# First products started on column quarters of the memory, with filler products ahead of them, and the squares of memory and x in other places

## The reference

```python
mem_n = rmsnorm(mem, mem_norm)                  # 256 memory tokens x 2048
for layer in range(2):
    h = rmsnorm(x, g[0]); mix = even_mixer(...) or odd_mixer(...)
    x = x + rmsnorm(mix, g[1])
    h = rmsnorm(x, g[2])
    k = mem_n @ wk[layer]; v = mem_n @ wv[layer]   # inside memory_cross_attention
    x = x + rmsnorm(memory_cross_attention(h, mem_n, wq, wk, wv, wo), g[3])
    h = rmsnorm(x, g[4]); x = x + rmsnorm(swiglu(h, ...), g[5])
```

## Time and profile before

| | before |
|---|---|
| median of 3 runs | 2846.91 us (2846.89 to 2847.23) |
| the profiled execution | 2846.54 us |
| its span in the trace | 2844.8 us, so 1.7 us lie around it |
| PE busy | 2826.8 us, 99% of the span |
| DVE busy | 2207.7 us, 78% |
| ACT busy | 1586.4 us, 56% |
| weights and other data moved | 593 MB, 208 GB/s mean |

### The profile page before, as it was taken

One profiled execution on the slowest core, in us unless ns is written; L12 is line 12 of the kernel. 1 busy time (PEld: TensorE's weight loads), 2 busy tenths in 40 slices (PEclk: granted clock), 3 DMA queues, 4 the chain that ended last, 5 costly groups with the idle time before them and its releaser, 6 DMA issues. The chain is left out here.

```text
span 2844.8 us, 31833 instructions
## 1 busy us (share of the span) xinstructions
PE 2826.8 (99%) x12990; PEld 2346.7 (82%) x12990; DVE 2207.7 (78%) x1517; ACT 1586.4 (56%) x1432; POOL 53.0 (2%) x109
## 2 busy tenths in 40 slices
PE   9999999999999999999999999999999999999998
PEld 7888888888888888888888888778888888888887
DVE  7888787669699988885456877899599888986444
ACT  7666555546356655664444765556456656655443
POOL 0000000000000000000000000000000000000000
PEclk9999999999999999999999999999999999999999
DMA  7674754656466546547555654656566556456552
GB/s 273 230 279 168 275 198 176 244 181 243 177 221 237 184 173 235 214 170 282 192 193 174 214 192 167 237 188 236 205 214 223 183 215 232 170 190 271 195 194 94
DMA packets 240241, 593.01 MB, mean 208 GB/s; under 512 B 9009, under 2 KB 9041, under 8 KB 223585
## 3 DMA queue, kind: packets, MB, share of 16 engines
q1 hardware_dynamic: 233792, 532.72, 52.5%
q0 software_dynamic: 5424, 47.78, 4.3%
q10 hardware_dynamic: 880, 10.49, 0.9%
HBM read 569.98 MB, written 20.97 MB: 208 GB/s over the span
## 5 line engine op out<-in xcount | busy, mean ns | idle before, releaser
L1183 DVE TENSOR_TENSOR w_lo<-wide,w_hi 128x2048 fp32r<-128x2048 f32 x556 | 1261.8, 2290 | 371.4 <-ACT w_hi L604 367.8
L604 ACT ACTIVATE w_hi<-wide 128x2048 fp32r<-128x2048 f32 x556 | 1060.2, 1915 | 478.6 <-PE ps L1934 367.3
L1934 PE MATMUL ps<-w_hi,act_hi 128*128 128x512 f32 x3272 | 877.3, 391 | 0.3 <-ACT w_hi L617 0.2
L1934 PE MATMUL ps<-w_lo,act_hi 128*128 128x512 f32 x3272 | 872.3, 389 | 0.9 <-DVE w_lo L1183 0.9
L1934 PE MATMUL ps<-w_hi,act_lo 128*128 128x512 f32 x3272 | 871.3, 389 | 0.0
L1934 PEld LDWEIGHTS ps<-w_lo,act_hi 128*128 128x128 f32 x3272 | 613.9, 188 | 130.5 <-DVE w_lo L1183 3.1
L1934 PEld LDWEIGHTS ps<-w_hi,act_lo 128*128 128x128 f32 x3272 | 614.4, 188 | 128.1
L1934 PEld LDWEIGHTS ps<-w_hi,act_hi 128*128 128x128 f32 x3272 | 611.9, 188 | 127.9 <-issue 1.9
L1187 DVE TENSOR_TENSOR wide<-wide,wide 128x2048 f32<-128x2048 f32 x114 | 261.1, 2290 | 5.6 <-DVE w_sum L1187 0.5
L1138 ACT ACTIVATE act_hi<-mid 128x256 fp32r<-128x256 f32 x80 | 33.4, 418 | 243.1 <-PE ps L1934 243.1
L604 ACT ACTIVATE w_hi<-w_sum 128x2048 fp32r<-128x2048 f32 x38 | 73.0, 1922 | 102.3 <-DVE w_sum L1187 90.7
(11 more groups left out here) (266 smaller groups left out, 1655.2 us busy)
## 6 DMA issues: line engine op xcount, KB each, us to landing
wide<-in_ffn_w_gate SPq DMA_DIRECT2D x88, 1024.0 KB, 8.4
wide<-in_ffn_w_up SPq DMA_DIRECT2D x88, 1024.0 KB, 7.3
wide<-in_ffn_w_down SPq DMA_DIRECT2D x88, 1024.0 KB, 4.8
wide<-in_odd_w_in SPq DMA_DIRECT2D x48, 1024.0 KB, 5.6
wide<-in_xattn_wk SPq DMA_DIRECT2D x32, 1024.0 KB, 7.8
wide<-in_xattn_wv SPq DMA_DIRECT2D x32, 1024.0 KB, 6.7
wide<-in_even_w_in SPq DMA_DIRECT2D x32, 1024.0 KB, 6.8
wide<-in_xattn_wq SPq DMA_DIRECT2D x32, 1024.0 KB, 5.5
```

The costliest lines, as they stand in the source:

```text
L604: nc.scalar.activation(w_hi[:, c % W_SLOTS, :], src, ACT.Copy).then_inc(hi_done, 2)
L1183: nc.vector.tensor_tensor(w_lo[:, c % W_SLOTS, :], src, w_hi[:, c % W_SLOTS, :].bitcast(F32), ALU.subtract).then_inc(lo_done, 2)
L1934: return nc.tensor.matmul(dst, lhs, rhs, start=start, stop=stop, skip_group_check=loose)
```

## The change

It has three parts. **Fillers:** PE issues products of a tile of ones into bank 0, of which nothing is kept: 4 ahead of the gain vectors' product, 3 ahead of the first transposes, 6 behind them. **Quarters:** the memory comes in four column quarters of 512 KB with both token halves, each ahead of its chunk; chunk 0 comes in two halves. PE turns tiles 4s to 4s+3 of both token halves (two tiles of 256 tokens to a bank), and in the new `opening_mem` takes each chunk for both token halves at once. ACT and DVE alternate two tiles of memory with half a chunk. **Squares:** ACT squares memory half 0 between chunks 2 and 3, half 1 behind chunk 3 as before; DVE takes the two `var` of the memory behind the first token sums instead of ahead of chunk 4. The squares of x go behind the splits of chunk products 8 and 10 of strip 1.

```diff
 # SP, in load(n, src)
-                if n == 1:
-                    for b in range(1, 4):
-                        memory(b)
-                    sp.wait_ge(mem_in[1], 16)
-                elif n < WIDE and n:
+                if 2 <= n < WIDE:
                     sp.wait_ge(wide_full[n - 2], 16)
-                if n == 3:
-                    sp.dma_start(memx[:, 1, :], mem[P:2 * P, :]).then_inc(mem_in[4], 16)
+                if n < 4:
+                    memory(n)
...
+                if n == 0:
+                    sp.dma_start(dst[:, 0:2, :], src[:, 0:2, :]).then_inc(first_half, 16)
+                    dst, src = dst[:, 2:4, :], src[:, 2:4, :]
 # ACT
-            def round_mem(m, banks=range(4)):
+            def round_mem(b, halves):
                 act.wait_ge(vec_done, 1)
...
+                for j in range(2):
+                    bank = WORK + 2 * (b % 2) + j
+                    act.wait_ge(work_full[bank], plan["mem_norm"]["rf"] + b // 2 + 1)
+                    for k in range(2):
+                        t = 4 * b + 2 * j + k
+                        ins = nc.scalar.activation(act_hi[:, t, :], ps[:, bank, k * T:(k + 1) * T], ACT.Copy,
+                                                   scale=vec[:, 16 + t:17 + t])
                     ins.then_inc(hi_ev, 1)
+                    split_halves(halves, b, (j,))
...
-            round_mem(1)
+            for s in range(4):
+                round_mem(s, first)
+                if s == 2:
+                    for landed_mem in mem_in:
+                        act.wait_ge(landed_mem, 16)
+                    square_x(0, memx, hx)
             act.dma_start(y[:], x.rearrange("(m p) n -> p m n", p=P)).then_inc(x_in, 16)
-            for m in range(MT):
-                square_x(m, memx, hx)
+            square_x(1, memx, hx)
...
+                if l == 0:
+                    take_k = transposed("mk0", kx, mv[0], before_9=x_square(0),
+                                        at_end=x_square(1), scale=rst_mem, pre="mem_norm")
 # DVE
+                take_k = transposed(f"mk{l}", kx, mv[0], before_6=nothing if l else x_roots, scale=rst_mem)
                 if l == 0:
-                    for m in range(MT):
-                        x_root(m)
-                take_k = transposed(f"mk{l}", kx, mv[0], second=x_roots if l == 0 else nothing,
-                                    scale=rst_mem)
+                    take_last, take_k = take_k, lambda: (take_last(), x_roots())
 # PE
+            def opening_mem(st):
+                c, pl = st.c, plan["mem_norm"]
+                for m in range(MT):
+                    pe.wait_ge(bank_free[m], st.u + 1)
+                for s in range(4):
+                    for ms in ((0, 1),) if s < 3 else ((0,), (1,)):
+                        for parts in (HI_HI, LO_HI, HI_LO):
+                            for k in range(4):
+                                if ms[0] == 0 and k % 2 == 0:
+                                    if parts is HI_HI:
+                                        pe.wait_ge(hi_ev, hi_ev_at["mem_norm"] + 2 * s + k // 2 + 1)
+                                        pe.wait_ge(hi_done, 2 * (c + s) + k // 2 + 1)
...
+                            if s < 3 and parts is (HI_HI if s else LO_HI):
+                                transposed_mem(s + 1)
...
+            def warm(n):
+                for _ in range(n):
+                    mm(ps[:, 0, 0:P], ones[:], ones[:])
             pe.wait_ge(consts_done, 4)
+            warm(4)
             pe.wait_ge(small_in, 48)
...
+            warm(3)
             transposed_mem(0)
+            warm(6)
```

More of the change, by code:

```diff
@@ L285, in build @@
         x_again = sem("x_again")
-        mem_in = [sem(f"mem_in{b}") for b in range(4)] + [sem("mem_in_other")]
+        mem_in = [sem(f"mem_in{b}") for b in range(4)]
+        first_half = sem("first_half")
         pv_done = sem("pv_done")
@@ L608, in split, with split_halves @@
                 hi(st.c + s, landed(st.n + s))
-            def split_halves(st, s):
+            def split_halves(st, s, halves=range(2)):
                 c = st.c + s
                 act.wait_ge(w_used, c + 1)
-                src = landed(st.n + s)
-                for h in range(2):
+                if c == 0:
+                    act.wait_ge(first_half, 16)
+                    src = wide[0][:]
+                else:
+                    src = landed(st.n + s)
+                for h in halves:
+                    if c == 0 and h:
+                        landed(0)
                     part = slice(h * HALF, (h + 1) * HALF)
@@ L892, in _, with x_square, run @@
             nc.scalar.activation(xrec[:, 0, :], half[:, 0:2], ACT.Copy)
[L893 to L897, removed]
-            round_mem(1)
-            act.dma_start(y[:], x.rearrange("(m p) n -> p m n", p=P)).then_inc(x_in, 16)
-            for m in range(MT):
-                square_x(m, memx, hx)
-            def x_squares():
-                act.wait_ge(x_in, 16)
-                for m in range(MT):
+            for s in range(4):
[4 more added lines that the diff above has]
+                    square_x(0, memx, hx)
+            act.dma_start(y[:], x.rearrange("(m p) n -> p m n", p=P)).then_inc(x_in, 16)
+            square_x(1, memx, hx)
+            def x_square(m):
+                def run():
+                    act.wait_ge(x_in, 16)
                     square_x(m, y, hx)
+                return run
             for l in range(LAYERS):
@@ L910, in _ @@
                 mv = plan[f"mv{l}"]["strips"]
-                take_k = transposed(f"mk{l}", kx, mv[0], second=x_squares if l == 0 else nothing,
-                                    scale=rst_mem, pre="mem_norm")
+                if l == 0:
+                    take_k = transposed("mk0", kx, mv[0], before_9=x_square(0),
+                                        at_end=x_square(1), scale=rst_mem, pre="mem_norm")
+                else:
+                    take_k = transposed(f"mk{l}", kx, mv[0], scale=rst_mem, pre="mem_norm")
                 def store_k():
@@ L1578, in _, with rest_mem @@
             dve.sem_inc(bank_free[4], 1)
-            def rest_mem(m, banks=range(4)):
+            def rest_mem(b, halves):
                 e0 = hi_ev_at["mem_norm"]
[L1583 to L1586, removed]
-                        ins = nc.vector.scalar_tensor_tensor(
[L1588 to L1594, removed]
-                split(first, s, (0, 1))
-            rest_mem(1)
+                for j in range(2):
+                    bank = WORK + 2 * (b % 2) + j
+                    dve.wait_ge(hi_ev, e0 + 2 * b + j + 1)
+                    for k in range(2):
+                        t = 4 * b + 2 * j + k
+                        ins = nc.vector.scalar_tensor_tensor(
+                            out=act_lo[:, t, :], in0=ps[:, bank, k * T:(k + 1) * T], scalar=vec[:, 16 + t:17 + t],
+                            in1=act_hi[:, t, :].bitcast(F32), op0=ALU.mult, op1=ALU.subtract)
+                    ins.then_inc(bank_free[bank], 1)
+                    split(halves, b, (j,))
+            for s in range(4):
+                rest_mem(s, first)
             def x_roots():
@@ L2118, in transposed @@
                     if st.g is None:
-                        opening(name, source, turned_by[source])
+                        if source == "mem_norm":
+                            opening_mem(st)
+                        else:
+                            opening(name, source, turned_by[source])
                         quad(st, 1, turned(0))
@@ L2136, in output, with transposed_mem @@
                     strip11(second, name, at_end=next_norm(nxt))
[L2138 to L2146 removed]
+            def transposed_mem(b):
+                pe.wait_ge(mem_in[b], 16)
+                for k in range(4):
+                    bank = WORK + 2 * (b % 2) + k // 2
+                    if k % 2 == 0:
+                        emptied(bank, plan["mem_norm"], b // 2)
+                    for m in range(MT):
+                        ins = nc.tensor.transpose(ps[:, bank, (k % 2) * T + m * P:(k % 2) * T + (m + 1) * P],
+                                                  memx[:, m, (4 * b + k) * P:(4 * b + k + 1) * P], ident[:])
+                    if k % 2:
+                        ins.then_inc(work_full[bank], 1)
```

31 lines of the change are left out of this document (14 added, 17 removed).

## The result

| | before | with the change |
|---|---|---|
| median of 20 runs | 2847.04 us (2846.41 to 2848.73) | 2850.84 us (2849.88 to 2852.22) |
| ratio, 95% interval | | 1.0013 [1.0007, 1.0019] |
| the profiled execution | 2846.54 us | 2850.24 us |
| its span | 2844.8 us | 2848.5 us |

The change made the kernel 3.8 us slower. That is under the 0.2% that I called telling from no change, but over the high end of my range by 2.1 us and on the other side of "before": I had forecast 0.7 us less. The interval leaves out 1, so the loss is real. The 20 launches with the change stand in two groups, ten from 2849.88 to 2850.60 us and ten from 2851.08 to 2852.22; the median lies between them, and the profiled execution belongs to the lower one.

A forecast was written before the change was run, and what follows sets the result against it. PE, busy 99% of the span, was the bound, so only its idle or slow time counted. Opening -2.4, late roots +2.5, squares of x -0.8 made -0.7 us: 2846.2 us, range 2844.2 to 2848.7.

The forecast's parts named there:

- POOL's two roots, 1.09: On POOL behind the memory's two `var`: both roots take 1.09 us, ending at 41.1.
- The chain's start: On DVE behind chunk 4's `w_hi`: `w_lo` of chunks 4 and 5 and four token sums end at 39.6.
- +2.5: Behind chunk 4: PE waits for the late roots and copies to `nat`, giving back 2.5 us.
- The clock in the pause: PE's 2.5 us pause at 40.0: a lost clock level costs 0 to 2.15 us; taken as 0.
- the clock falls in the new pause: Rival for PE's pause behind chunk 4: +2.15 us, giving 2848.3; chance 0.10.
- My worst case: Both clock cases together, in the opening and in the pause: 3.5 us slower.
- The opening: From the start to chunk 4: fillers and quarters start chunk 4 at 34.5 against 36.95, gaining 2.4 us.
- The stops: PE's waits for ACT in chunks 0 and 1 of the opening: 0.6 us idle in each.
- the second rival: The clock stays low through chunk 0's first pass, PE's first eight products: price 2.0 us, giving 2848.2; chance 0.15.
- The squares of x: Strip 1: moving them off ACT removes PE's stop ahead of 72.13, gaining 0.8 us; new places cost nothing.
- The squares of the memory: On ACT among chunks 2 to 4: each takes 1.9 us, with chunk 4's `w_hi` still ahead of PE's need.

The follow-up runs named there:

- root_alone: The change, with DVE waiting for both roots of the memory before its next subtraction; 2847.46 us, ratio 1.0002.
- late_var_only: The kernel before, with only DVE's two `var` of the memory moved behind the first token sums; 2851.08 us, ratio 1.0014.
- no_fill: The change without any of its 13 filler products; 2851.73 us, ratio 1.0017.
- early_no_fill: early_var without the filler products; 2845.14 us, ratio 0.9994.
- pause_filled: The change with 18 more filler products, into bank 7, where PE waits for the copies to `nat`; 2848.48 us, ratio 1.0006.
- early_turn: early_var with chunk 1's transposes one pass earlier, behind chunk 0's hi x hi pass; 2843.37 us, ratio 0.9987.
- early_var: The change with DVE's two `var` of the memory put back ahead of chunk 4; 2844.14 us, ratio 0.9991.
- var_between: The change with the two `var` between DVE's subtractions of chunks 4 and 5; 2844.21 us, ratio 0.9991.

## Why the prediction was wrong

**The step that failed** is the term of the chain "POOL's two roots, 1.09". I saw that the `var` would be late and uncovered, and priced the roots by a row with other neighbours. In the earlier trace rows the first root had DVE to itself, and no row there says what a root costs beside a long subtraction. Here the `var` stand directly ahead of `w_lo` of chunk 6, which starts 0.2 us before POOL does, and the roots take 3.12: +2.0 (shown by root_alone, where DVE's work beside them is taken away and they take 1.07). late_var_only has the same 3.12 in the old opening.

**The chain's start.** I had the token sums end at 39.6; they ended at 40.34, 0.75 later. It goes back to the start of the opening. I had the memory's first quarter land near 5.2, the 256 KB that it has more at the 2.6 to 2.7 us a MB of the later chunks. Without fillers in its way PE started on it at 5.95 (no_fill; 5.88 in early_no_fill). The view of stretches of the changed kernel fits that in its last column, GB/s: 214 from 2 to 6 us, on the mean, against 390 from 6 to 8.

```profile
2.00:6.00 4.00, 3.76 (x15) 3.50 (x16) 0.19 (x1) 1.24 (x2) 0.46 (x3) 1.00 0.76 214
6.00:8.00 2.00, 2.00 (x11) 2.00 (x11) 0.00 (x0) 0.62 (x2) 0.00 (x0) 1.00 1.04 390
```

The lateness then runs through the chain at nearly the same size: transposes at 6.22 and not 5.6, ACT's first pair at 7.38 and not 6.8, the first product at 9.41 and not 8.7, the square of memory half 1 at 29.51 and not 28.8. With the 2.0 this puts the transposes at 45.35 instead of 42.5, and the term "+2.5" is +4.5 (40.9 to 45.35).

**The clock in the pause.** I gave it bounds of 0 to 2.15 and took 0, from a pause of 0.56 us that had left the level; it fell and cost 1.65 (the granted clock of 0.50; pause_filled takes it away). This was the rival "the clock falls in the new pause", to which I gave 0.10. It didn't need the first error: late_var_only's pause is 2.51 us, the length that I had forecast, and the rate fell behind it too. My worst case had both clock costs, but with the pause at 2.5. The three together, 2.0 + 0.75 + 1.65, are 4.4, and carry the forecast of 2846.2 to 2850.6.

**The opening** gained 1.5 us in this launch and not 2.4. The fillers held the first transposes to 6.22, 0.3 behind no_fill's 5.95, which waited for the landing alone (I had 0.4). 0.7 of the missing 0.9 is the lateness of the landing. The rate rose around 8.3, not 6.6, so that all eight transposes were slow (0.21 apart), but this isn't what held the first product back. In early_turn's launch, with the same PE program up to there, the rate rose within the transposes, and the product still waited for ACT until 9.25:

```profile
6.22 1.43 PE L2157 MATMUL ps<-ident,memx 128*128 128x128 f32 x8
...
9.25 1.16 PE L1942 MATMUL ps<-w_hi,act_hi 128*128 128x512 f32 x4 [0.26 <-ACT w_hi L623]
```

The stops, 0.41 and 0.50 for ACT's second half, were as worked out (0.6 each): each group of four starts 0.67 later than the full rate would have it. That a lower rate stays longer was the second rival; its place, the eight first products, was wrong in this launch, and right where the fillers were gone. One reading of mine was off, though nothing rests on it: the four products of before between 10.78 and 12.63 are 0.46 each, and not the 0.43 of no_fill's eight. Of the opening's 0.9 us shortfall nothing reached the end by itself, as PE waited at 40.9 for the chain; it is in the chain's 0.75.

The Trainium skill, "TensorE: Matmul & The Clock Gate" (section on the PE-mode transpose), which I had weighed for that rival, says that a transpose does not count as PE's being busy in the way a product does; by it the transposes would break what the fillers built up. In the changed kernel's launch the fillers right behind the slow transposes were fast, in early_var's they were still slow, and in early_turn's the rate rose within the transposes: no run here settles it.

**The squares of x** gained 0.8 as predicted, and their new places cost nothing. **The squares of the memory** on ACT cost nothing either; early_var keeps them.

That the roots' slowness is DVE's doing is shown. By what it is done is argued: three subtractions of 2.28 us in the change, in late_var_only and in var_between made a root of 2.51, and the `rst_both` root ended 0.4 behind each, while a second root beside token sums of 0.7 us took 0.63 against 0.55. The Trainium skill, "SBUF — State Buffer" (section "SBUF: two separate sides"), says that DVE and GpSimd share a pair of ports which an instruction of either holds alone to its end, among others a DVE operation with two inputs in SBUF against a GpSimd one that reads there. This fits: the subtraction has two such inputs, started first (40.50 against 40.68), and the root ended after it. The 0.08 that the token sums cost a root, with two such inputs as well, doesn't follow from that rule as it stands. The prediction didn't apply it to a root.

**Open:** why the rate rises at 8.3 in one launch, at 10.4 in another and near 7 in a third of the same opening, and when a pause makes it fall. Pauses of 4.32, 4.29 (no_fill) and 2.51 us did so in their profiles, one of 2.28 didn't. It may vary from launch to launch. The kernels with an idle pause behind chunk 4 spread over 2.3 to 3.4 us, and early_turn, early_var, var_between and pause_filled, which have none, over 0.2 to 0.8. Of the upper ten launches of the change nine show a mean granted clock of 0.998, the lower ten all 0.999. But a pause there is not the only source: early_no_fill has none and spreads over 3.5 us, before over 2.3 in 20 launches, and the late weight chunk of early_no_fill cost 1 us. No profile shows a launch of the upper group.

## What to carry to other kernels

A duration is read with its neighbours: before a small POOL instruction's time is put into a chain, look for what DVE starts right behind the instruction that releases it, and give it DVE's time where the two overlap. When a covered step is moved into the open, every link of its chain has to be priced again for the new place, and the pause that it makes can have a second price, the clock's. Where two costs follow from one event (a longer wait and a slower engine after it), they belong in one case of the range. A first transfer is priced at the rate of the start of the launch, and not at that of the steady stream behind it.

## What the hardware showed that I had not expected

- A root on 128 x 1 numbers took 0.55 us alone and 2.51 to 2.60 beside a subtraction of 2048 columns. The changed kernel has it a second time, in the view of the tile `rstd`, where nothing waits for it:

```profile
L479 POOL TENSOR_TENSOR rstd<-var,half x2: 548/1570/2592, 116.6 to 119.2; 128x1 f32<-128x1 f32 x2
```

- Filler products in a pause of 4.3 us took 2.0 to 2.4 us off the median (by the ratios and by the medians; 1.74 between the profiled executions) and nine tenths off the spread, though they compute nothing.
- The granted clock of the view of stretches is not to be trusted at the start of a launch. This is no_fill's row from 10 to 12 us, where its products are 0.43 apart:

```profile
10.00:12.00 2.00, 2.00 (x6) 1.40 (x5) 2.00 (x4) 0.63 (x1) 0.00 (x0) 1.00 1.05 394
```

  It reads 1.00 there, and 0.50 for the same spacing at 47 us in the changed kernel. At the start only the spacing of equal products tells the level.
